# Gate and up products with both halves of the activations as one moving operand

## The reference, cut to what matters

```python
D_FF = int(math.ceil(D_MODEL * 8 / 3 / 256) * 256)        # 2816

def swiglu(h, w_gate, w_up, w_down):
    return (jax.nn.silu(h @ w_gate) * (h @ w_up)) @ w_down
...
        h = rms_norm_2(x, g_pre_ffn[i])
        x = x + rms_norm_2(swiglu(h, w_gate[i], w_up[i], w_down[i]), g_post_ffn[i])
```

## Time and profile before

| | |
|---|---|
| median of 3 runs | 816.75 us (816.7 to 818.13) |
| the profiled execution | 817.35 us, its span 815.5 us |
| PE busy | 750.4 us, 92% of the span, 5438 matmuls |
| PE weight loads | 622.9 us, 76% |
| DVE busy | 401.6 us, 49% |
| ACT busy | 332.6 us, 41% |
| DMA | 203.99 MB, 250 GB/s in the mean |

### The profile page before, as it was taken

How to read it: one execution, slowest core, us unless ns; L and a number is a source line. 1 busy time by engine, 2 the same in 40 slices (tenths; PEclk the granted TensorE clock), 3 DMA queues, 4 the chain that set the end, 5 groups by cost and what they waited for, 6 DMA issues and landing times.

```text
span 815.5 us, 12982 instructions
## 1 busy us (share of the span) xinstructions
PE 750.4 (92%) x5438; PEld 622.9 (76%) x5438; DVE 401.6 (49%) x730; ACT 332.6 (41%) x597; POOL 23.8 (3%) x45
## 2 busy tenths in 40 slices
PE   8989999999999999996866868999998999999996
PEld 7888787888888885552443446999878999999995
DVE  5747755666758531110100108566657655565554
ACT  5476465455444331110110105556546444444442
POOL 1100000000000000000000002100002000000000
PEclk9999999999999999998989989999999999999998
DMA  9637365635987879999999999954343554556101
GB/s 337 208 130 197 138 220 191 221 131 168 380 322 254 344 315 423 420 420 421 420 421 422 420 401 354 364 201 155 121 139 126 184 200 162 194 170 204 53 1 52
DMA packets 83691, 203.99 MB, mean 250 GB/s; under 512 B 6960, under 2 KB 47536, under 8 KB 71088
## 3 DMA queue, kind: packets, MB, share of 16 engines
q1 hardware_dynamic: 83632, 203.15, 67.2%
HBM read 202.09 MB, written 1.05 MB: 249 GB/s over the span
## 4 chain that ended last, share of the span: by engine, by line
PE 77%; DMA 10%; DVE 4%; ACT 3%; issue 2%; SPq 1%; POOL 1%; DVEq 0%; ACTq 0%; POOLq 0%
PE ps L582 57%; DMA ext<-in_w_gate_e 7%; PE ps L863 5%; DMA big<-in_w_up_e 3%; PE ps L884 2%; PE ps L842 2%; PE ps L897 2%; DVE wl L1442 1%; SPq L451 1%; PE ps L945 1%; PE ps L563 1%; ACT junk L1097 1%; PE ps L959 1%; PE ps L973 1%; PE ps L760 1%
## 5 line engine op out<-in xcount | busy, mean ns | idle before, releaser
L1442 DVE TENSOR_TENSOR wl<-raw,wh 128x1024 fp32r<-128x1024 f32 (+3 forms) x180 | 213.5, 1200 | 138.6 <-ACT wh L1088 138.4
L1088 ACT CAST wh<-raw 128x1024 fp32r<-128x1024 f32 (+3 forms) x180 | 183.1, 1031 | 101.3 <-PE ps L582 101.2
L582 PE MATMUL ps<-fra,wh 128*128 128x256 f32 x1168 | 213.7, 285 | 5.9 <-DVE fra L1868 2.6
L582 PEld LDWEIGHTS ps<-fra,wh 128*128 128x128 f32 x1168 | 183.8, 193 | 8.3 <-DVE fra L1868 2.8
L582 PE MATMUL ps<-wh,fra 128*128 128x512 f32 (+3 forms) x668 | 188.8, 368 | 0.7 <-DVE gb L1654 0.4
L582 PE MATMUL ps<-fra,wl 128*128 128x256 f32 x584 | 166.0, 284 | 0.0
L582 PEld LDWEIGHTS ps<-wh,fra 128*128 128x128 f32 x668 | 118.9, 189 | 19.6 <-DVE wl L1442 1.5
L582 PE MATMUL ps<-wl,fra 128*128 128x512 f32 (+3 forms) x334 | 121.3, 363 | 0.0
L582 PEld LDWEIGHTS ps<-fra,wl 128*128 128x128 f32 x584 | 112.7, 193 | 0.0
L863 PE MATMUL ps<-ext,big 128*32 128x256 f32 x480 | 53.8, 446 | 23.0 <-DMA ext<-in_w_up_e 10.7
L582 PE MATMUL ps<-wh,frb 128*128 128x512 f32 x240 | 74.4, 391 | 0.0
(11 more groups left out here) (240 smaller groups left out, 809.8 us busy)
## 6 DMA issues: line engine op xcount, KB each, us to landing
ext<-in_w_up_e SPq DMA_DIRECT2D x23, 1024.0 KB, 26.1
raw<-in_w_in SPq DMA_DIRECT2D x16, 1024.0 KB, 5.1
raw<-in_w_gate_e SPq DMA_DIRECT2D x16, 1024.0 KB, 9.9
raw<-in_w_down_e SPq DMA_DIRECT2D x16, 1024.0 KB, 27.0
raw<-in_w_qkv SPq DMA_DIRECT2D x12, 1024.0 KB, 12.8
raw<-in_w_gate SPq DMA_DIRECT2D x11, 1024.0 KB, 5.2
raw<-in_w_up SPq DMA_DIRECT2D x11, 1024.0 KB, 5.1
raw<-in_w_down SPq DMA_DIRECT2D x11, 1024.0 KB, 4.9
```

The source lines that it names most:

```text
L582: t = e.matmul(o, a, w, start=first and n == 0, stop=final and n == 2, skip_group_check=not check)
L1088: e.copy(halves(q)[0], piece_view(q)).then_inc(*up("wh", q))
L1442: e.tensor_tensor(l, piece_view(q), h.bitcast(F), ALU.subtract).then_inc(*up("wl", q))
```

## The change

Gate and up get a matmul routine of their own, `joint`, in place of `features`. The two halves of the activations are laid side by side, so that for each row k 512 columns lie together: 256 tokens of the high half, then 256 of the low (`hT_both`). The tile `wh` meets all 512 in one matmul and fills a whole bank; `wl` meets the 256 of the high half and adds into that bank's first half. For each row the wide products of both tiles j are issued first, then the two narrow ones. Each tile j has a bank of its own: gate always takes banks 4 and 5, up always 6 and 7, in every chunk. The two halves of each bank have to be added afterwards: DVE does it with `tensor_reduce`, once per bank, into `S[0]` for gate and `S[1]` for up, and the multiplications that read the banks now read `S`.

```diff
-    hT = [fra[:, a:a + 2048].rearrange("p (t n) -> p t n", t=8) for a in (0, 2048)]
+    hT = [fra[:, 0:4096].rearrange("p (t z n) -> p z t n", t=8, z=2)[:, z] for z in range(2)]
+    hT_both = fra[:, 0:4096].rearrange("p (t m) -> p t m", t=8)
...
+        def joint(key, banks, freed, ready=(), later=(), row=None):
+
+
+            for q in wt.run[key]:
+                p = wt.pieces[q]
+                h, l = halves(q)
+                for point in ready if p.k0 == 0 else later if p.k0 == 4 else ():
+                    e.wait_ge(*point)
+                e.wait_ge(*at("wl", q))
+                for kk in range(p.rows):
+                    k = p.k0 + kk
+                    if row:
+                        e.wait_ge(*at(*row, k))
+                    cols = [slice(P * j, P * j + P) for j in range(len(banks))]
+                    for j, b in enumerate(banks):
+                        if k == 0:
+                            enter(b, *freed, j)
+                        e.matmul(bank[b][:, :], h[:, kk, cols[j]], hT_both[:, k], start=(k == 0), stop=(k == 7),
+                                 skip_group_check=True)
+                    for j, b in enumerate(banks):
+                        t = e.matmul(bank[b][:, 0:256], l[:, kk, cols[j]], hT[0][:, k], start=False, stop=(k == 7),
+                                     skip_group_check=True)
+                t.then_inc(*up("piece", q))
+                yield
...
-                whole(features(("fg", c), 4 + 2 * (c % 2), hT, ("scaled gate", c), row=("lo", "ffn") if c == 0 else None))
-                whole(features(("fu", c), 5 + 2 * (c % 2), hT, ("a", c)))
+                whole(joint(("fg", c), (4, 5), ("summed gate", c), row=("lo", "ffn") if c == 0 else None))
+                whole(joint(("fu", c), (6, 7), ("summed up", c)))
...
+        def summed(name, c, q, dst, banks):
+
+            e.wait_ge(*at("piece", q))
+            for j, b in enumerate(banks):
+                e.tensor_reduce(dst[:, j, :], bank[b][:, :].rearrange("p (z n) -> p n z", z=2), AX, ALU.add).then_inc(
+                    *up("summed " + name, c, j))
+
+        rows = krow.unsqueeze(1).to_broadcast([P, 2, 256])
+
         def scaled_gate(c):
             if c:
                 e.wait_ge(*at("al", c - 1))
-            e.wait_ge(*at("piece", last["fg", c]))
-            e.tensor_tensor(S[0].rearrange("p (j n) -> p j n", j=2),
-                            bank[4 + 2 * (c % 2)][:, :].rearrange("p (j n) -> p j n", j=2),
-                            krow.unsqueeze(1).to_broadcast([P, 2, 256]), ALU.mult).then_inc(*up("scaled gate", c, 0))
+            summed("gate", c, last["fg", c], two_of(S[0]), (4, 5))
+            e.wait_ge(*own())
+            e.tensor_tensor(two_of(S[0]), two_of(S[0]), rows, ALU.mult).then_inc(*up("scaled gate", c, 0))
...
-                e.wait_ge(*at("piece", last["fu", c]))
+                summed("up", c, last["fu", c], two_of(S[1]), (6, 7))
+                e.wait_ge(*own())
                 e.wait_ge(*at("silu", c, 0))
-                e.tensor_tensor(S[1], S[0], bank[5 + 2 * z][:, :], ALU.mult).then_inc(*up("a", c, 0))
+                e.tensor_tensor(S[1], S[0], S[1], ALU.mult).then_inc(*up("a", c, 0))
```

More of the change, by code:

```diff
@@ L1964, in vector, with two_of @@
         split_to(wt.run["o", 3][1] + AHEAD)
+        def two_of(v):
+            return v.rearrange("p (j n) -> p j n", j=2)
+        def summed(name, c, q, dst, banks):
[4 more added lines that the diff above has]
+        rows = krow.unsqueeze(1).to_broadcast([P, 2, 256])
         def scaled_gate(c):
```

## The result

| | before | after |
|---|---|---|
| median of 20 runs | 818.04 us (816.65 to 818.89) | 815.37 us (813.61 to 816.93) |
| the profiled execution, its span | 817.35, 815.5 | 815.25, 813.5 |
| PE matmuls, busy | 5438, 750.4 us | 5086, 745.3 us |
| DVE instructions, busy | 730, 401.6 us | 774, 427.6 us |

The ratio is 0.9969, with an interval of 0.9962 to 0.9976: 2.5 us faster. The changed kernel was compared a second time: 0.9971 (0.9958 to 0.9984). I call its profile from there the second one.

The account below looks back on a forecast made before the run. The prediction took PE's start-to-start times in the feed-forward as the bound. Products gaining 3.8 us and a bank wait costing 2.1 gave -1.7 us, so 815.05 us from a median of 816.75; range 812.8 to 817.6.

Parts of the forecast that it names:

- PE's products: Gate and up: a group (two wide, two narrow products) takes 698 ns, 720 before; 176 groups gain 3.9 us.
- run-in: On PE, where wide products follow narrow ones: the first wide ones together take some 0.03 us longer.
- Rivals A: Gate and up products on PE: no run-in, a group takes 686 to 694 ns, 814.4 to 812.9 us; chance 0.25.
- B: Gate and up products on PE: full run-in at every group, 710 ns, 817.1 us, no change; chance 0.17.
- Rival D: Gate and up products: cost per matmul mostly not removed, a group about 715 ns, 818.05 us; chance 0.04.
- Why 13 ns: PE's products: wide and narrow both pay 13 ns on top of their columns, a cost per matmul, not per column.
- Chunk 0: First chunk, ahead of `spread`: its gain on PE arrives almost whole, less 0.1 us, leaving 3.8 of 3.9.
- The sums: DVE's four `tensor_reduce` per chunk: 0.70 us each, 2.8 us per chunk, all hidden in the middle chunks.
- The bank wait: Between chunks 0 and 1: PE waits once for DVE's gate sums of chunk 0 to free the banks, 2.1 us.
- The last chunk: Last down products: `al` ends at about 801.0 us, PE arrives at about 801.8, so hidden by 0.8 us.

Follow-up runs that it names:

- Experiment 4: The changed kernel with each wide product made as two narrow ones of 256 columns into the halves of the same bank; ratio to before 1.0016.
- experiment 11: The changed kernel with each narrow product of 256 columns made as two of 128 with the same weights; 855.5 us in one execution.
- experiment 8: The changed kernel with each `tensor_reduce` on DVE made twice in a row; 825.0 us in one execution.
- 2: The changed kernel with chunk 1's gate products in banks 0 and 1; 813.01 us, ratio to before 0.994.
- 3: The kernel before with gate always in bank 4 and up always in bank 5, no turns; ratio to before 1.0019.
- 9: The kernel before with four copies of one element per chunk added to DVE's program; 816.21 us in one execution.
- 5: The changed kernel with each tile's narrow product behind its wide one (wide, narrow, wide, narrow); ratio to before 1.0.

## Why the prediction was right

The forecast was 1.7 us, all from the feed-forward. The 2.5 us measured are made of more than I had; the stage itself gave 2.30 us undisturbed (4.2 from PE's products less 1.9 of the wait), by the path that I described.

- *PE's products.* I forecast 698 ns for a group, between 694 and 702. It measured 697 in the timeline; over nine chunks (161.89 less 158.33 is 3.56 us in 144 groups) 695 with the borders to the down products. Gain 4.1 to 4.3 instead of 3.9. That part of the run-in is paid and part given back was the right picture, though not place by place: in the middle chunks both wide products of a group take 233 ns and not only the first, and the narrow ones 115 and 116. Rivals A (686 to 694) and B (710) are out. Experiment 4 ties the whole gain to the operand. Rival D is out too: 23 to 25 ns for two matmuls less are 12 each. The Trainium skill, TensorE: Matmul & The Clock Gate, section "Wait — 56ns, not 53.3ns?", with its 2.5 ns per warm matmul, does not hold for these operands.
- *Why 13 ns.* I called it a cost per matmul. Between 256 and 512 columns the sum came out, but experiment 11 shows that it is no law: the step "it is a cost per matmul, not per column" was too wide.
- *Chunk 0.* Its gain should arrive less 0.1: it gained 0.27 of 0.37. Right.
- *The sums.* 0.70 forecast, 0.65 a piece in a pair (1.29 for two), 683 ns alone. A reduce with elements 256 apart costs as one with neighbours. Hidden in the middle chunks, as worked out; a chunk lasts 16.58, forecast 16.63. The margin was real and thin: experiment 8 uses it up.
- *The bank wait.* 2.1 forecast, 1.58 + 0.30 = 1.9 measured, the cheaper reduces being most of the difference (two of 0.65 for two of 0.72); place, releaser and single occurrence as forecast (2, 3).
- *The last chunk.* `al` was ready at 799.5 and PE came to the last down products at 800.9: 1.4 us to spare, where I had 0.8. DVE was less late than I had it: it started the up sums at 796.1, 0.5 us behind the end of PE's last up product (795.6), where I had 0.9 (797.4 against some 796.5 in the old times); the two cheaper reduces gave another 0.1.
- *Not foreseen: the clock.* The idle 1.33 us can be followed by 3.4 us at 1.2 GHz, 1.56 us lost; it was in one of the two profiles of this kernel. The stage then gives 0.74 instead of 2.30. Of the eight other profiles of kernels with this bank wait and no work put into it, one more has such a fall there (experiment 8), and one has it 2 us into chunk 1 (experiment 11); none of the four without the idle time has one. That the idle time causes it is likely and not shown.
- *Not foreseen: the tail.* 0.77 us, from DVE's longer program, nothing to do with the idea of the change (9).

Undisturbed, 2.30 + 0.77 = 3.1 us, with a fall of the clock 1.5; the measured 2.5 and 2.4 lie between. The timed runs lie in groups: before 816.65 to 817.19 (9 runs) and 817.95 to 818.89 (11), after 813.61 to 814.21 (5), 815.20 to 815.95 (14) and 816.93 (1). Between the means of the two lower groups lie 2.9 us, and between the 11 and the 14 again 2.9. A fall of the clock near 45 us, which has nothing to do with the change, is worth about this distance of 1.5 us, and a fall at chunk 1 too, so a time alone does not tell which of them a run had. How often the clock falls at chunk 1 stays unknown.

Two things in how close the prediction came are luck. Its two missing terms pull in opposite directions: 0.8 us gained in the tail, and up to 1.6 lost at the clock. And its 815.05 us started from a median of three runs, 816.75, two of them in the lower group; the 20 runs gave 818.04. From there 1.7 us less would have been 816.3, and 815.37 was measured: the forecast gain was too small by 0.8 us (by the ratio), not by the 0.3 that the two medians seem to show, and the 1.7 lies outside the interval of the ratio (2.0 to 3.1 us).

## What to carry to other kernels

On a bound PE, price an order of matmuls by start-to-start times, and look at both borders of each kind: two wide and two narrow kept the gain, one and one lost about half of it. When a change takes away the turns of banks or frees them later, look for the one place where the next tenant follows without other work between: here it ate 1.9 of 4.2 us, and two free banks gave it back (ratio 0.994). For a difference of 0.1%, look also at what a longer or shorter program does to its own code fetches, and at where the granted clock fell in the two executions, before it is put down to the idea.

## What the runs showed of the hardware

- float32r products with their own 128 x 128 weights start 120 ns (256 columns) and 227 ns (512) apart in rows of their kind. With 128 columns they start 111 ns apart in the middle of a row of four. The Trainium skill, TensorE: Matmul & The Clock Gate, section "Back-to-back issue gap", gives some 81 ns for 128 columns in a stream of weight loads and matmuls; these runs show 111.
- Where both kinds mix, wide products take 6 to 9 ns more than in a long row and narrow ones give 3 to 5 ns back: 233 and 115 to 116 ns in groups of two and two, 236 and 117 one by one (means of the middle chunks). Alternating one by one costs 10 ns per four.
- The granted clock fell to 0.50 for 3.4 us behind an idle time of 1.33 us in one execution and not in another of the same kernel; in the profiles of three other kernels (experiments 4, 5 and 11) it fell at the start of chunk 0, behind idle stretches of 0.5 to 1.1 us while the norm ahead of it is made.
- With one fetch of instructions of 8 KB among the output's writes these landed 2.6 us behind their issue, 2.1 without it, and the end came 0.77 us later.
